# Two-layer decoder step on one core: probabilities in three buffers, stores first, rotary swap and value order by DMA

## The reference, cut to what matters

```python
def rope(x, pos):                       # 16 of a head's 64 features are rotated
    xr = x[..., :ROT_DIM]
    x1, x2 = xr[..., :half], xr[..., half:]
    rot = concatenate([x1 * cos - x2 * sin, x2 * cos + x1 * sin])
    return concatenate([rot, x[..., ROT_DIM:]])
...
for g, (w, d) in enumerate(((128, 1), (512, 4), (2048, 16))):     # mixer B
    win = dynamic_slice(kv_pad[g], t0, w + Q_BLOCK)
    loc = dilated_offsets(w, Q_BLOCK, w, d)
    stats.append(dilated_stats(qb[:, :, g], win[:, loc], (t0 - w + loc) >= 0))
```

## Time and profile before

| what | us |
|---|---|
| median of 3 runs (lowest, highest) | 2430.18 (2427.51, 2432.29) |
| the profiled execution | 2428.99 |
| its span | 2427.2 |
| projections of A, two stretches | 42.3 and 68.3 |
| attention of A | 180 |
| projections of B | 88 |
| values of B | 65 |
| memory pairs and dilated pairs of B | 22 and 80 |

### The profile page before, as it was taken

One profiled execution on the slowest core, in us unless ns is written; L12 is line 12 of the kernel. 1 busy time (PEld: TensorE's weight loads), 2 busy tenths in 40 slices (PEclk: granted clock), 3 DMA queues, 4 the chain that ended last, 5 costly groups with the idle time before them and its releaser, 6 DMA issues.

```text
span 2427.2 us, 43261 instructions
## 1 busy us (share of the span) xinstructions
PE 2253.6 (93%) x17601; PEld 2096.8 (86%) x17601; DVE 1066.3 (44%) x1465; ACT 708.5 (29%) x879; POOL 341.5 (14%) x299
## 2 busy tenths in 40 slices
PE   6999999998756889999999999999998789999997
PEld 6999999868423379999999999999997459999997
DVE  7333335448945734333345333335422225333344
ACT  5232224221422123332234332224113324332222
POOL 2110011313311001100111110111421102110111
PEclk9999999999867999999999999999999999999998
DMA  6224423303200533233234223324223031223212
GB/s 242 90 82 148 142 91 119 105 18 116 61 1 7 188 102 130 100 130 117 97 112 160 87 101 112 126 101 138 73 83 132 14 122 65 92 82 108 88 63 77
DMA packets 57077, 243.94 MB, mean 101 GB/s; under 512 B 7346, under 2 KB 28346, under 8 KB 39938
## 3 DMA queue, kind: packets, MB, share of 16 engines
q1 hardware_dynamic: 49330, 204.41, 24.4%
q10 hardware_dynamic: 7632, 37.92, 4.4%
HBM read 234.73 MB, written 34.80 MB: 111 GB/s over the span
## 4 chain that ended last, share of the span: by engine, by line
PE 83%; DVE 11%; ACT 2%; issue 2%; ACTq 1%; POOL 1%; DMA 0%; SPq 0%; DVEq 0%; POOLq 0%
PE ps L500 74%; DVE tk L1514 2%; PE ps L714 2%; DVE work L1517 1%; PE ps L733 1%; DVE pbuf L1454 1%; DVE wl L1235 1%; PE ps L701 1%; PE ps L657 1%; PE ps L878 1%; PE ps L693 1%; ACT wh L954 1%; DVE tkw L1517 1%; DVE xl L1248 0%; DVE a_sc L1584 0%
## 5 line engine op out<-in xcount | busy, mean ns | idle before, releaser
L500 PE MATMUL ps<-xh,wh 128*128 128x260 f32 x3296 | 671.3, 285 | 4.9 <-DVE memv L1288 3.3
L500 PE MATMUL ps<-xh,wl 128*128 128x260 f32 x3296 | 666.2, 284 | 0.0
L500 PE MATMUL ps<-xl,wh 128*128 128x260 f32 x3296 | 665.3, 284 | 0.0
L1235 DVE TENSOR_TENSOR wl<-raw,wh 128x2048 fp32r<-128x2048 f32 x181 | 416.2, 2300 | 361.7 <-ACT wh L954 361.7
L500 PEld LDWEIGHTS ps<-xh,wh 128*128 128x128 f32 x3296 | 512.6, 189 | 6.8 <-DVE memv L1288 3.5
L500 PEld LDWEIGHTS ps<-xh,wl 128*128 128x128 f32 x3296 | 510.3, 189 | 0.0
L500 PEld LDWEIGHTS ps<-xl,wh 128*128 128x128 f32 x3296 | 508.7, 189 | 0.0
L954 ACT ACTIVATE wh<-raw 128x2048 fp32r<-128x2048 f32 x181 | 344.7, 1906 | 371.4 <-PE ps L500 355.7
L500 PE MATMUL ps<-acth,wh 128*128 128x260 f32 x1600 | 324.6, 284 | 6.8 <-ACT acth L1198 4.3
L500 PE MATMUL ps<-actl,wh 128*128 128x260 f32 x1600 | 324.9, 284 | 0.0
L500 PE MATMUL ps<-acth,wl 128*128 128x260 f32 x1600 | 323.9, 284 | 0.0
(11 more groups left out here) (210 smaller groups left out, 1948.1 us busy)
## 6 DMA issues: line engine op xcount, KB each, us to landing
raw<-in_w_ffn_in SPq DMA_DIRECT2D x88, 1024.0 KB, 4.8
raw<-in_w_ffn_out SPq DMA_DIRECT2D x32, 768.0 KB, 4.3
raw<-in_w_ffn_out SPq DMA_DIRECT2D x32, 640.0 KB, 3.9
raw<-in_w_in_b SPq DMA_DIRECT2D x10, 1024.0 KB, 4.7
raw<-in_w_in_a SPq DMA_DIRECT2D x9, 1024.0 KB, 4.8
out_state<-in_state ACTq DMA_DIRECT2D x8, 1022.0 KB, 5.9
ring_w<-in_kpool SPq DMA_DIRECT2D x40, 128.0 KB, 2.2
raw<-in_w_mem SPq DMA_DIRECT2D x4, 1024.0 KB, 7.0
```

The lines of the kernel that those rows point to most:

```text
L500: mm = pe.matmul(o, w(kt), moving, start=(kt == 0 and i == 0), stop=(kt == nk - 1 and i == 2))
L1235: dve.tensor_tensor(wl[:, n % 2, :], raw[:, n % 2, :], wh[:, n % 2, :].bitcast(F32), ALU.subtract)\
```

## The change

Three things are changed. (1) The swap of the rotated features is no longer a product: SP copies, for each roped tile, four strips of 8 partitions from `tiles` into `tu`, which GpSimd has zeroed; VectorE multiplies `tu` by `sinf` in place, GpSimd adds from there. SP's new `swaps(M, i)` stand behind the load of chunk i and handle tiles 2i-4 and 2i-3. (2) In mixer B the values of groups 1 and 2 are computed for plain token blocks into `b_nat`, and SP's 32 DMAs bring them into the order by residue in `b_v`; TensorE and ScalarE wait for them (`v_moved`) ahead of the dilated pairs, and the store of `v_b` moves there. (3) The place of a pair's probabilities in `pbuf` goes by u % 3 in place of u % 2 for pairs of up to 512 columns, and VectorE's step k begins with the store of pair k-2. Left out below: the declarations of semaphores, the dropped load of `rot`, and its count in three waits.

```diff
@@ -187,6 +186,9 @@
...
         b_vs = placed("b_vs", [8, 3, 256], F32, VALUES_AT + 3072)
+
+        b_nat = [None, tiles[:, 14:16, :].rearrange("p a t -> p (a t)")[:, 0:1024].rearrange("p (b c) -> p b c", c=256),
+                 work[:, 0:1024].rearrange("p (b c) -> p b c", c=256)]
         b_mask = [scs[:, 0:768], tkw[:, 0:768]]
@@ -270,10 +273,10 @@
...
                 q.update(u=u, s_at=[h * 1024 if wide else (u % 2) * 1024 + h * 512 for h in range(2)],
-                         p_at=[(u % 2) * 1536 + h * 768 if wide else (u % 2) * 1024 + h * 512 for h in range(2)],
+                         p_at=[(u % 2) * 1536 + h * 768 if wide else (u % 3) * 1024 + h * 512 for h in range(2)],
                          s_range=(0, 2048) if wide else ((u % 2) * 1024, (u % 2) * 1024 + 1024),
                          p_range=((u % 2) * 1536, (u % 2) * 1536 + 1536) if wide else
-                         ((u % 2) * 1024, (u % 2) * 1024 + 1024), groups=[])
+                         ((u % 3) * 1024, (u % 3) * 1024 + 1024), groups=[])
                 tiles_of = [(t, h) for t in range(q["cols"] // P) for h in range(2)]
@@ -303,6 +306,7 @@
...
         Q_PLACED = {"idx": 16, 0: 20, 1: 32, 2: 36, 3: 48}
+        V_MOVED = 16 * 2 * NBLK * 4
         Q_ZEROED = {1: 1, "idx": 2, 0: 3, 3: 4, 2: 5}
@@ -419,6 +423,21 @@
...
                     n += count + KT
+            def swaps(M, i):
+
+                for t in (2 * i - 4, 2 * i - 3):
+                    if t not in M["roped"]:
+                        continue
+                    k = M["rope0"] + M["roped"].index(t)
+                    sp.wait_ge(raw_ready, M["tile0"] + t + 1)
+                    sp.wait_ge(swap_zeroed, M["layer"] + 1)
+                    if k >= 2:
+                        sp.wait_ge(roped, k - 1)
+                    for h in (0, HD):
+                        for to, at in ((h, h + HD // 8), (h + HD // 8, h)):
+                            sp.dma_start(tu[to:to + HD // 8, k % 2, :], M["tiles"][t][at:at + HD // 8, :])\
+                              .then_inc(swapped[k % 2], 16)
+
             def ring_loads(kind, what, layer):
                 for it in items:
@@ -450,6 +469,7 @@
...
                 load(plan["in_a"] + i, ins["w_in_a"][i])
+                swaps(mixers[0], i)
             for i in range(2):
@@ -461,8 +481,14 @@
...
                 load(plan["in_b"] + i, ins["w_in_b"][i])
+                swaps(mixers[1], i)
             for i in range(2):
                 load(plan["out_b"] + i, ins["w_out_b"][i])
+            for g in (1, 2):
+                for blk in range(NBLK):
+                    sp.wait_ge(v_done, mixers[1]["v0"] + 5 * g + blk + 1)
+                    for r in range(4):
+                        sp.dma_start(b_v[32 * blk:32 * blk + 32, g, r, :], b_nat[g][r:P:4, blk, :]).then_inc(v_moved, 16)
             for r in range(2):
@@ -629,7 +655,7 @@
...
-                for t in range(first, last + 1):
+                for t in range(first, last):
                     if t < last:
@@ -646,17 +672,6 @@
...
                             rms(norm, 6, 4)
-                    if t > first and t - 1 in M["roped"]:
-                        k = M["rope0"] + M["roped"].index(t - 1)
-                        pe.wait_ge(raw_ready, T0 + t)
-                        if k >= 1:
-                            pe.wait_ge(sin_ready, k)
-                        if t == 1:
-                            pe.wait_ge(rms_read, norm + 1)
-                        for h in range(2):
-                            mm = pe.matmul(ps[:, 6 + h, 0:TH], rot[:, :], M["tiles"][t - 1][:, h * TH:(h + 1) * TH],
-                                           start=True, stop=True)
-                        mm.then_inc(rot_ready, 1)
@@ -672,8 +687,8 @@
...
                     done, _ = v_block_done(M, i)
-                    product([ps[0:rows, 2 * (i % 3), 0:256]], lambda kt: xh[:, kt, tokens(tb, g)],
-                            lambda kt: xl[:, kt, tokens(tb, g)], lambda kt: [wh[:, n % 2, kt * 256:(kt + 1) * 256]],
+                    product([ps[0:rows, 2 * (i % 3), 0:256]], lambda kt: xh[:, kt, tokens(tb, 0)],
+                            lambda kt: xl[:, kt, tokens(tb, 0)], lambda kt: [wh[:, n % 2, kt * 256:(kt + 1) * 256]],
                             lambda kt: [wl[:, n % 2, kt * 256:(kt + 1) * 256]], KT).then_inc(done, 1)
@@ -935,6 +950,7 @@
...
             attend(1, pairs[1][:8])
+            pe.wait_ge(v_moved, V_MOVED)
             attend(1, pairs[1][8:])
@@ -1069,9 +1085,9 @@
...
                     act.wait_ge(rtok_ready, (M["norm"] + 2) // 3)
-                    rows, col = NSAMP if tb == 4 else P, rtok_col(tb, g)
+                    rows, col = NSAMP if tb == 4 else P, rtok_col(tb, 0)
                     to = (a_vs[:, :] if tb == 4 else a_v[:, tb, :]) if M["layer"] == 0 else \
-                        (b_vs[:, g, :] if tb == 4 else b_v[:, g, tb, :])
+                        (b_vs[:, g, :] if tb == 4 else b_nat[g][:, tb, :] if g else b_v[:, g, tb, :])
                     act.activation(to, ps[0:rows, 2 * (i % 3), 0:256], ACT.Copy, scale=rtok[0:rows, col:col + 1])\
@@ -1082,8 +1098,7 @@
...
                 else:
-                    stores = ((outs["k_b"], tiles[:, 6:12, :]), (outs["v_b"], b_v[:, :, :, :]),
-                              (outs["vs_b"], b_vs[:, :, :]))
+                    stores = ((outs["k_b"], tiles[:, 6:12, :]), (outs["vs_b"], b_vs[:, :, :]))
                 for to, src in stores:
@@ -1219,6 +1234,8 @@
...
             attend(pairs[1][:8])
+            act.wait_ge(v_moved, V_MOVED)
+            act.dma_start(outs["v_b"], b_v[:, :, :, :]).then_inc(out_written, 16)
             attend(pairs[1][8:])
@@ -1369,11 +1386,8 @@
...
                     k = M["rope0"] + M["roped"].index(t)
-                    dve.wait_ge(rot_ready, k + 1)
-                    if k >= 2:
-                        dve.wait_ge(roped, k - 1)
-                    dve.tensor_tensor(halves(tg[:, k % 2, :]), bank2(6), halves(sinf[:, :]), ALU.mult)\
-                       .then_inc(sin_ready, 1)
+                    dve.wait_ge(swapped[k % 2], 64 * (k // 2 + 1))
+                    dve.tensor_tensor(tu[:, k % 2, :], tu[:, k % 2, :], sinf[:, :], ALU.mult).then_inc(sin_ready, 1)
@@ -1475,6 +1489,8 @@
...
                     masked(q)
                 for k, q in enumerate(us):
+                    if k >= 2:
+                        store(us[k - 2])
                     if k + ahead < len(us):
                         masked(us[k + ahead])
@@ -1482,8 +1498,6 @@
...
                     if extra:
                         extra(k)
-                    if k >= 2:
-                        store(us[k - 2])
                 for q in us[-2:]:
                     store(q)
@@ -1739,14 +1753,16 @@
...
             def ropes(M):
+                pool.wait_ge(ssum_done, KT * (M["norm"] + 1))
+                pool.memset(tu[:, :, :], 0.0).then_inc(swap_zeroed, 1)
                 for j, t in enumerate(M["roped"]):
                     k = M["rope0"] + j
                     tile = M["tiles"][t]
-                    pool.wait_ge(rot_ready, k + 1)
+                    pool.wait_ge(swapped[k % 2], 64 * (k // 2 + 1))
                     pool.tensor_tensor(tile, tile, cosf[:, :], ALU.mult).then_inc(cos_ready, 1)
                     pool.wait_ge(cos_ready, k + 1)
                     pool.wait_ge(sin_ready, k + 1)
-                    pool.tensor_tensor(tile, tile, tg[:, k % 2, :], ALU.add).then_inc(roped, 1)
+                    pool.tensor_tensor(tile, tile, tu[:, k % 2, :], ALU.add).then_inc(roped, 1)
             def diagonals(us):
```

More of the change, by code:

```diff
@@ L155, in build @@
         sinf = sb("sinf", [P, T])
-        rot = sb("rot", [P, P])
         ident = sb("ident", [P, P])
@@ L237, in build @@
         mkv_done = sem("mkv_done")
-        t_ready = sem("t_ready"); raw_ready = sem("raw_ready"); rot_ready = sem("rot_ready")
+        t_ready = sem("t_ready"); raw_ready = sem("raw_ready"); swapped = [sem("swapped0"), sem("swapped1")]; swap_zeroed = sem("swap_zeroed")
         sin_ready = sem("sin_ready"); cos_ready = sem("cos_ready"); roped = sem("roped")
@@ L256, in build @@
         ot_head = sem("ot_head"); ot_rest = sem("ot_rest")
+        v_moved = sem("v_moved")
         bmask_loaded = [sem("bmask_loaded0"), sem("bmask_loaded1")]
@@ L388, in _ @@
             sp.dma_start(y[:, :, :], ins["x"]).then_inc(y_loaded, 16)
-            for t, src in ((cosf, "cos"), (sinf, "sin"), (rot, "rot"), (causal, "causal")):
+            for t, src in ((cosf, "cos"), (sinf, "sin"), (causal, "causal")):
                 sp.dma_start(t[:, :], ins[src]).then_inc(rope_loaded, 16)
@@ L924, in _ @@
             A, B = mixers
-            pe.wait_ge(rope_loaded, 16 * 4)
+            pe.wait_ge(rope_loaded, 16 * 3)
             tiles_in(A, 0, 6)
@@ L1680, in _ @@
             ffn(0)
-            dve.wait_ge(rope_loaded, 16 * 4)
+            dve.wait_ge(rope_loaded, 16 * 3)
             tiles_in(A, 0, 6)
@@ L1768, in _ @@
```

(2 more changed lines are left out.)

## The result

The changed kernel takes 2320.47 us (median; 2318.01 to 2322.16) against 2430.02 us beside it on the same chip: ratio 0.9549, interval 0.9532 to 0.9565, so 109.6 us less. Forecast were 2333 us (2319 to 2353), 97.3 us less. The direction, the range and the order of the terms held; the gain is 12 us larger than the sum. The profiled execution has a span of 2317.4 us.

The account below looks back on a forecast made before the run. TensorE, busy 93% of the span, was taken as the bound, trading waits with VectorE in layer A's attention; terms of 4.0, 3.5, 10.5, 22.3, 48.5, 0.5 and 8.0 sum to 97.3 us, giving 2333 us (2319 to 2353).

Parts of the forecast that it names:

- all four places: Where time can move: both layers' projections, B's value products, A's attention with the search after it, B's dilated pairs.
- A's attention: Layer A's heavy attention: store first and third buffer remove the 53.1 us of mask waits; 48.5 us gained.
- TensorE keeps its mix of clocks: Layer A's attention: granted clock stays 0.67, TensorE's 58.6 us of work remain, gain 45.6 us.
- VectorE binds: Layer A's attention: TensorE stays at 2.4 GHz, its work shrinks and VectorE sets the time, gain 53 us.
- a little more everywhere: Whole kernel: every upper bound of the terms taken, 2323 us; chance 0.08.
- theory P: Attention: mask and weighing waits are separate; order alone gives about 2418 us, buffer alone 2380 us.
- the stall only moves: Layer A's attention: the store at the front waits for its own pair's products, nothing gained there, 2381 us; chance 0.03.
- TensorE cold: Layer A's attention: TensorE more often at 1.2 GHz, stretch about 68 us, gain 36, 2345 us; chance 0.15.
- Swap: Both layers' projections: 25 rotation products replaced by DMAs, 18.0 us gained; swap there 6.4 us after the raw tile.
- Values: Layer B's values: eight blocks without the token step of four, each 2.79 us shorter, 22.3 us gained.
- The rival that a page's rule gave: Layer B's values: fp32 strides up to 4 elements are free, so the term is 0, 2355 us; chance 0.04.
- The moved store of v_b: Layer B's attention: the 1.5 MB store leaves its crowded start, nobody waits for it until the rows, 0 us.

Follow-up runs that it names:

- Run 3: The kernel before with the store first and the third probability buffer, rotary and values as before: 2366.45 us, ratio 0.974.
- Runs 1 and 2: The kernel before with only the store first: 2372.22 us; the kernel before with only the third probability buffer, store still last: 2410.42 us.
- the two-piece run: The changed kernel with each swap DMA cut in two by columns, 8 per tile, same bytes: 2336.05 us, ratio 0.9622.
- run 4: The kernel before with only layer B's values made in natural token order and put in residue order by 32 DMAs: 2406.57 us.
- run 8: The changed kernel with layer B's second value group taking every second token and the third every third: 2328.83 us.
- runs 1, 2, 3 and 5: The last of these, 5, is the kernel before with the rotary swap by DMA alone: 2407.44 us, ratio 0.9918.
- run 12: The changed kernel as it is, measured again beside another run on the same chip: 2321.8 us, ratio 0.9562.
- run 11: The changed kernel; in layer A's attention alone, ScalarE copies the inverse sums and GpSimd makes the negated maximum: 2308.25 us.

## Why the prediction was right, and where its sizes were off

- **What bounds where.** Right at all four places. The product stream, B's values and the search behind A's attention hand every microsecond on: the 66.8 us gained by the end of A's search are still there in full at B's projections (67.3).
- **A's attention, 48.5 us forecast, 57.4 measured**, above even the upper bound of 53. This term carries most of the difference of 12 us. The value was taken between "TensorE keeps its mix of clocks" (45.6) and "VectorE binds" (53); the second is what happened, granted clock 0.92. By the masks of the same pairs (673.13 and 763.95 us before, 660.93 and 699.95 after; the last stores at 777.53 and 710.71) the stretch of 104.4 us became 49.8, 54.6 us less. The other 2.8 us were gained ahead of it, where the term allowed nothing. Run 3, without the swap, has the same 2.8. This term alone takes the time below the rival "a little more everywhere" as well, whose 2323 us should be 2324: its bounds add up to 105.9 us.
- **The mechanism of that term was only half understood.** The text gives the 53.1 us to the buffer and sees the store as a detail beside it (4.65 us for a wait), though the same trace has fourteen waits for the store, 52.0 us. Runs 1 and 2 show one loop through both engines: the order alone brings 56 of 62 us, the buffer alone 18 (by the end of A's search 50.5, 19.5 and, with both, 56.8 us). The term came out because the change makes both edits; by the same reading, the forecasts for the order alone and the buffer alone (theory P) were off by 46 and 30 us.
- **The rivals "the stall only moves" and "TensorE cold"** fell with the windows above: 49.0 us for the stretch, against 68 in the cold case.
- **Swap.** First six tiles 4.6 to 5.0 against 4.0, last ten 4.8 against 3.5, B 10.6 against 10.5. Tiles are 5.77 us apart, and TensorE waits for no split. Its price was wrong: 1.09 us of queue was taken from the issue of a store of 8 partitions, and the copies cost 0.62 to 0.67; the swap is there 4.2 us after the raw tile (issue of the first at 1690.87, GpSimd's next product at 1695.09), not 6.4. With the price as forecast, the two-piece run would have cost 73 us; it cost 16. That VectorE sometimes takes 2.9 to 3.4 us for a split beside GpSimd's additions harmed nobody.
- **Values.** 22.3 forecast, 22.1 measured, and 22.0 in run 4. The rival that a page's rule gave (the Trainium skill, SBUF — State Buffer, the note on cachelines) fell. The same note of the page also says that a line has 16 bytes and that two hits on it are needed for full speed. Worked out for fp32, that makes a step of two free and one of three or four not, and run 8 agrees (2.84, 2.88, 4.18 us a block, 5.63 in the earlier trace rows's kernel), though no run here shows that lines are the cause. The conclusion of four elements, which the prediction quoted, is one that the measurement refutes.
- **The moved store of v_b, put at zero**, is the one step that failed outright, by about 1 us: the text named the queue it moves to and not the one it leaves, where the first exponential stood behind it. This is half of the 1.9 us where 0.5 was forecast for the memory pairs; the other half goes with a granted clock of 0.92 against 0.85, which the runs don't tie to the store.
- **Dilated pairs.** 8.0 forecast, 7.2 measured; the wait for the store went in five of eight pairs (7.1 us), and the little clock that I added didn't come.
- **Slower by late copies** needed a landing time of 13 us. Copies inside SBUF of 8 partitions are there some 1.5 us after the last is issued.

In run 3 the mask of the sample comes 56.75 us earlier than before and the end of B's values 54.97. The 1.8 us lost between are within the 2.1 us by which two traces of the changed kernel differ there. Not settled: what sets the granted clock in the memory pairs, which came out at 0.92 and at 1.00 for one and the same kernel.

## To carry to other kernels

When two engines wait for each other in turn, follow one pair round the loop, with every instruction that stands between one wait's end and the other's, before you give each wait to a cause: here the loop of 10.4 us, followed instruction by instruction, told roughly what either edit alone would bring (49 and 24 us, for 56 and 18 measured), and the totals of the waits did not. For each step that is moved, price the queue that it leaves as well as the one that it joins. And once the stall is gone, look at which engine is full at that place: work taken from it pays there and costs elsewhere, so move it only in the stage where that engine binds.

## What the runs showed of the hardware

- A small copy from SBUF to SBUF costs SP's queue 0.62 us to issue and 0.67 us from one to the next, for 16, 8 and 5 KB alike, and the work that needs four of them began 4.2 us after the first was issued. The 32 KB copies of the values took 0.59 us to issue (median of 32, the changed kernel) and landed 1.8 us after.
- TensorE's weight load of 128 by 128 fp32: 188 ns with tokens next to each other, 197 at every second, 262 at every third, 332 at every fourth. Products of 256 columns come 117 to 120 ns apart at the first two, 174 at three, 234 at four.
- The issue of the same small store by ScalarE (24 KB) took 0.87 to 1.11 us behind the store of v_b (the kernel before and runs 1, 2, 3 and 5) and 0.58 without it.
- Four passes over 512 columns took 2.08 us in the kernel before, where TensorE waited 4.39 to 4.65 us in every pair, and 1.13 in the changed kernel. There, with no wait over a microsecond up to the last scores, the granted clock in A's heavy attention rose from 0.67 to 0.92 (0.97 in run 12), and to 1.00 in run 11.
